# Expert retrieval in groups of 32 tokens with four heads side by side, and another order of key and weight transfers

## The reference

```python
h  = rmsnorm(x) * norm1 modulated by adaLN(c)            # 6 vectors of 1024 per request from c @ w_ada
z  = h @ w_in                                            # conv parts, q, k, v, indexer q, k, w, two gates
mix = sigmoid(ga) * (conv(z) @ w_convout) + sigmoid(gb) * (sparse_attention(z, cache) @ w_attnout)
x  = x + gate1 * (mix @ w_out)
h2 = rmsnorm(x) * norm2 modulated                        # the second half: retrieval
q  = (h2 @ w_q).reshape(t, 8 heads, 2, 128)              # w_q is 1024 x 2048
s  = q . sub_keys                                        # per head two lists of 128 scores
s1, i1 = top_k(s[:, :, 0], 16); s2, i2 = top_k(s[:, :, 1], 16)
e, g = best 16 of the 256 sums s1 + s2; e = i1 * 128 + i2; g = softmax(the 16 sums)
act = gelu(u_tab[e] . h2)                                # u_tab, v_tab: 16384 rows of 1024
y  = sum over 8 heads x 16 of (g * act) * v_tab[e]
out = x + gate2 * y
```

## Time and profile before

| | |
|---|---|
| median of three runs | 1093.47 us |
| the profiled execution | 1094.85 us, its span 1093.0 |
| TensorE busy | 950.8 us, 87% |
| VectorE busy | 715.6 us, 65% |
| ScalarE busy | 415.7 us, 38% |
| GpSimd busy | 286.2 us, 26% |
| moved from HBM | 377.75 MB, 347 GB/s over the span |
| queue of the gathers | 306.61 MB |

### The profile page before, as it was taken

How to read it: one execution, slowest core, us unless ns; L and a number is a source line. 1 busy time by engine, 2 the same in 40 slices (tenths; PEclk the granted TensorE clock), 3 DMA queues, 4 the chain that set the end, 5 groups by cost and what they waited for, 6 DMA issues and landing times.

```text
span 1093.0 us, 11438 instructions
## 1 busy us (share of the span) xinstructions
PE 950.8 (87%) x3288; PEld 487.2 (45%) x3288; DVE 715.6 (65%) x1775; ACT 415.7 (38%) x1120; POOL 286.2 (26%) x314
## 2 busy tenths in 40 slices
PE   4999999969999999999999877877877777777787
PEld 2457877646777655554454322322222222222222
DVE  1266879885647877676667787888864444444544
ACT  2112313101402555455466445345343333333333
POOL 0001000002001333343344333333333333333330
PEclk9999999989999999999999999899999999999999
DMA  9837352777536999999999999999999999999993
GB/s 367 326 120 263 116 198 87 251 294 273 194 127 259 390 416 418 421 420 419 421 419 420 420 419 421 420 419 419 420 420 420 421 420 420 420 419 420 421 420 152
DMA packets 63764, 380.08 MB, mean 348 GB/s; under 512 B 7651, under 2 KB 20115, under 8 KB 22358
## 3 DMA queue, kind: packets, MB, share of 16 engines
q0 software_dynamic: 42944, 306.61, 68.1%
q1 hardware_dynamic: 20470, 72.41, 17.6%
q10 hardware_dynamic: 288, 0.35, 0.1%
HBM read 377.75 MB, written 1.59 MB: 347 GB/s over the span
## 4 chain that ended last, share of the span: by engine, by line
DMA 44%; PE 41%; DVE 6%; ACT 4%; issue 2%; SPq 2%; POOL 0%; DVEq 0%; POOLq 0%; ACTq 0%
DMA big<-peer_uv,oT 39%; PE twoA L591 7%; PE twoD L956 7%; PE twoD L958 6%; PE twoA L895 4%; PE twoA L569 3%; PE twoD L829 3%; DMA big<-weight_rows 3%; DVE big L1851 2%; SPq L987 2%; DMA r<-peer_uv,oT 1%; PE twoD L817 1%; PE twoA L728 1%; PE twoA L511 1%; ACT big L1298 1%
## 5 line engine op out<-in xcount | busy, mean ns | idle before, releaser
L1089 POOL DMA_INDIRECT big<-peer_uv,oT x259 | 244.7, 945 | 484.8 <-PE twoD L958 379.2
L956 PE MATMUL twoD<-big 128*128 128x512 f32 x518 | 285.6, 633 | 98.2 <-ACT big L1298 98.1
L1851 DVE CUSTOM_DVE_ANT_0 big<-big,twoA 128x1024 f32<-128x1024 f32 x146 | 178.2, 1221 | 144.4 <-DMA big<-peer_uv,oT 143.1
L958 PE MATMUL twoD<-big 128*128 128x512 f32 x518 | 268.2, 600 | 0.0
L1293 ACT ACTIVATE oT<-oT,wsel 128x1 f32<-128x1 f32 x288 | 84.5, 293 | 323.0 <-DVE oT L1851 317.8
L956 PEld LDWEIGHTS twoD<-big 128*128 128x128 f32 x518 | 84.5, 191 | 269.8 <-ACT big L1298 232.8
L1851 DVE CUSTOM_DVE_ANT_0 big<-big,twoD 128x1024 f32<-128x1024 f32 x113 | 137.9, 1221 | 71.6 <-DMA big<-peer_uv,oT 68.8
L958 PEld LDWEIGHTS twoD<-big 128*128 128x128 f32 x518 | 99.7, 193 | 126.1 <-issue 126.1
L591 PE MATMUL twoA<-hT,big 128*128 128x288 f32 x448 | 115.3, 414 | 10.0 <-DMA big<-weight_rows 10.0
L1298 ACT ACTIVATE big<-ctab,oT 128x128 f32<-128x128 f32 x288 | 115.6, 401 | 9.5
L591 PEld LDWEIGHTS twoA<-hT,big 128*128 128x128 f32 x448 | 85.0, 193 | 36.7 <-DMA big<-weight_rows 10.9
(11 more groups left out here) (330 smaller groups left out, 952.5 us busy)
## 6 DMA issues: line engine op xcount, KB each, us to landing
big<-weight_rows SPq DMA_DIRECT2D x24, 2048.0 KB, 11.4
big<-weight_rows SPq DMA_DIRECT2D x8, 1024.0 KB, 4.9
big<-peer_uv,oT POOLq DMA_INDIRECT x259, 22.8
r<-key_rows SPq DMA_DIRECT2D x40, 64.0 KB, 2.0
big<-index_rows SPq DMA_DIRECT2D x64, 32.0 KB, 2.7
r<-weight_rows SPq DMA_DIRECT2D x1, 2048.0 KB, 12.1
big<-key_rows SPq DMA_DIRECT2D x24, 64.0 KB, 4.9
big<-weight_rows SPq DMA_DIRECT2D x1, 1312.0 KB, 14.3
```

The source lines that it names most:

```text
L956: pe.matmul(acc[0][:, :], diag[j % NDG], row[:, 0:512], start=(s == 0), stop=(s == SLOTS[t] - 1), skip_group_check=True)
L958: mm = pe.matmul(acc[1][:, :], diag[j % NDG], row[:, 512:D], start=(s == 0), stop=(s == SLOTS[t] - 1), skip_group_check=True)
L1089: pool.indirect_dma_start(pairs[home[i]], None, peer_uv, bass.IndirectOffsetOnAxis(ap=eidx[:, t, s:s + 1], axis=0)).then_inc(row_in[home[i ...
L1851: dve.tensor_tensor_reduce(out=row, in0=row, in1=h2tok[t][:, :], scale=1.0, scalar=0.0, op0=ALU.mult, op1=ALU.add, accum_out=dots[:, t, s: ...
```

## The change

1. **Groups.** All 288 tokens go in nine groups of 32, each with four heads in the four strips of 32 partitions: 9 x 32 slots, again 288 rounds. A unit is now four or eight heads of 32 tokens.
2. **Queries.** For group 0, `first_queries` computes rows: 32 tokens by 512 columns, in four strips, for two weight blocks at once, and turns them with `sum4`. Heads 0 to 3 come ahead of the first gather, 4 to 7 behind it. The sixteen blocks then run twice in the rounds: for tokens 32 to 127 in rounds 1 to 16, and for tokens 128 to 287 in every second round from 19 to 49.
3. **Values.** ScalarE writes a 128 x 32 matrix (`spread`); the two halves of v go to two neighbouring strips, other ones in the next round, and one PSUM bank holds a group's sums.
4. **h2** is spread to the four strips by 32 small matmuls per group (`spread_h2`), into one place, so it waits for the last dot of the group before.
5. **Group ends.** `scale_sums`, then `finish_group` adds the strips and x on TensorE; rows go out after every group.
6. **Ring.** 6 buffers, 8 from gather 27, 10 from 35, 12 from 43; the added ones lie in the weights `peerq` 0, 1 and 2.
7. **Transfers.** `peerq` 0 to 3 go to slots 0, 1, 5, 4 (before 5, 4, 0, 1). Keys of requests 0 and 1 are asked for after `convout`, of 2 and 3 after `gate` 7, of 7 after `adaG` 11.

```diff
-        ALL_ROWS, RING = 11, ((0, 7), (50, 9), (74, 11))
+        ALL_ROWS, RING = 12, ((0, 6), (27, 8), (35, 10), (43, 12))
-("peerq", 0, 5), ("peerq", 1, 4), ("peerq", 2, 0), ("peerq", 3, 1)]
+("peerq", 0, 0), ("peerq", 1, 1), ("peerq", 2, 5), ("peerq", 3, 4)]
-        BLOCK_AT = {4 + 6 * n: 5 + n for n in range(11)}
-        SCORE_AT = {5 + 12 * n: 2 + n for n in range(6)}
+        BLOCK_AT = {1 + n: (n, GTOK, P) for n in range(16)}
+        BLOCK_AT.update({19 + 2 * n: (n, P, TOK) for n in range(16)})
+        SCORE_AT = {17: 2}
+        SCORE_AT.update({GSLOTS * (n - 2) + 5: n for n in range(3, len(units))})
-            while unit < len(units) and i >= SCORED[unit] and n < (2 if unit < 4 else 1):
+            while unit < len(units) and i >= SCORED[unit] and n < (2 if unit < 3 else 1):
...
+            def first_queries(n):
+                for half in range(2):
+                    w, b = weights(pe, group("peerq", 2 * n + half)), A.open(pe)
+                    for k in range(DC):
+                        q = k % 4
+                        if n == 0:
+                            pe.wait_ge(h_ready, DC + k + 1)
+                        mm = pe.matmul(b[32 * q:32 * q + 32, :], hT[:, k, 0:GTOK], w[:, k, :], start=(k < 4), stop=(k >= 4),
+                                       skip_group_check=True)
+                    A.close(mm)
+                b = A.open(pe)
+                for half in range(2):
+                    pe.wait_ge(qrow_ready, 2 * n + half + 1)
+                    for j in range(4 * half, 4 * half + 4):
+                        mm = pe.matmul(b[:, GTOK * j:GTOK * (j + 1)], qrow[n][:, j * P:(j + 1) * P], cv["sum4"], start=True, stop=True)
+                A.close(mm)
+            first_queries(0)
             score_unit(0)
+            spread_h2(0)
...
+            first_queries(1)
+            score_unit(1)
...
+            def spread_h2(t):
+                if t:
+                    pe.wait_ge(u_used, GSLOTS * t)
+                for c in range(DC):
+                    for r in range(QUAD):
+                        mm = pe.matmul(h2rep[GTOK * r:GTOK * (r + 1), c * P:(c + 1) * P], hT[:, c, GTOK * t:GTOK * (t + 1)], ident,
+                                       start=True, stop=True)
...
+                if s == GSLOTS - 1 and t + 1 < GROUPS:
+                    spread_h2(t + 1)
+                pe.wait_ge(spread_ready, j + 1)
+                for half in range(2):
+                    r = (2 * j + half) % QUAD
+                    mm = pe.matmul(bankD[t % 2][GTOK * r:GTOK * (r + 1), :], spread[j % NDG],
+                                   pairs[home[j]][:, D + 512 * half:D + 512 * (half + 1)], start=(s < 2), stop=(s >= GSLOTS - 2),
+                                   skip_group_check=True)
                 mm.then_inc(v_used, 1)
...
+            def finish_group(t):
+                b = A.open(pe)
+                for c in range(DC):
+                    half = c // 4
+                    pe.matmul(b[GTOK * half:GTOK * (half + 1), c % 4 * P:(c % 4 + 1) * P], xT[:, c, GTOK * t:GTOK * (t + 1)], ident,
+                              start=(c % 4 == 0), stop=False, skip_group_check=True)
+                pe.wait_ge(ysum_ready, t + 1)
+                for half, of in enumerate(("even", "odd")):
+                    mm = pe.matmul(b[GTOK * half:GTOK * (half + 1), :], cv[of], ysum[:, t % 2, :], start=False, stop=True,
+                                   skip_group_check=True)
...
                 if g == group("convout"):
                     sp.wait_ge(*attended[0])
-                    for b in range(KB):
-                        load_keys(b)
+                    load_keys(0)
+                    load_keys(1)
+                if g == group("gate", 7):
+                    load_keys(2)
+                    load_keys(3)
+                if g == group("adaG", 1):
                     sp.wait_ge(a_ready, 1)
                     load_keys(NB - 1)
...
-                elif home[i] in (5, 6):
+                elif home[i] in (6, 7):
                     pool.wait_ge(*released[group("peerq")])
-                elif home[i] in (7, 8):
+                elif home[i] in (8, 9):
+                    pool.wait_ge(*released[group("peerq", 1)])
+                elif home[i] in (10, 11):
                     pool.wait_ge(*released[group("peerq", 2)])
-                elif home[i] in (9, 10):
-                    pool.wait_ge(*released[group("peerq", 3)])
```

More of the change, by code:

```diff
@@ L470, in layer_program @@
         NORM_AT = {ROUTED_AT[unit] + 3: unit for unit in range(1, len(units))}
+        assert all(ROUTED_AT[unit] + 3 <= first_slot[unit] for unit in range(1, len(units)))
         home, turn, before = [], [], []
@@ L861, in score_unit @@
-                A.close(mm)
-            def turn_h2(t):
-                pe.wait_ge(h_ready, 2 * DC + 2 if t else 2 * DC)
-                for q in range(DC):
-                    mm = pe.transpose(h2tok[t][:, q * P:(q + 1) * P], hT[:, q, t * P:(t + 1) * P], ident)
-                mm.then_inc(h2_ready, 1)
-            first = weights(pe, group("peerq"))
-            for j in range(2):
+                for i in range(nh):
+                    for r in range(QUAD):
+                        for q in range(2):
+                            head = QUAD * (h + i) + r
+                            mm = pe.matmul(b[GTOK * r:GTOK * (r + 1), (2 * i + q) * P:(2 * i + q + 1) * P],
+                                           qpT[:, 2 * head + q, GTOK * t:GTOK * (t + 1)], subT[:, q * PH + head, :], start=True, stop=True)
@@ L933, in _, with gate_rows @@
-            keep_busy(A, 4)
+                if end == TOK:
+                    released[g] = (a_full, A.n)
+            def gate_rows(t):
+                if t == 0:
+                    pe.wait_ge(bias_landed, 16)
+                    pe.wait_ge(g2sel_ready, 1)
+                    pe.wait_ge(adaG_ready, 2)
+                b = A.open(pe)
+                for r in range(QUAD):
+                    pe.matmul(b[GTOK * r:GTOK * (r + 1), :], g2sel[:, t * GTOK:(t + 1) * GTOK], adaG[:, r % 2, :], start=True, stop=False,
+                              skip_group_check=True)
+                for r in range(QUAD):
+                    mm = pe.matmul(b[GTOK * r:GTOK * (r + 1), :], ones[0:1, 0:GTOK], biasG[:, r % 2 * 512:(r % 2 + 1) * 512], start=False,
+                                   stop=True, skip_group_check=True)
+                A.close(mm)
@@ L1297, in weigh @@
                     act.wait_ge(v_used, j - NDG + 1)
[L1298 removed]
+                act.activation(spread[j % NDG], cv["sum4"], ACT.Copy, scale=w).then_inc(spread_ready, 1)
             def copy_query(j, a, e):
```

318 lines of the change are left out of this document (126 added, 192 removed).

## The result

| | before | changed |
|---|---|---|
| median of runs | 1093.28 us (1092.79 to 1094.33, 5 runs) | 1118.76 us (1118.33 to 1122.6, 5 runs) |
| profiled execution, its span | 1094.85, 1093.0 us | 1122.6, 1120.8 us |
| first gather issued | 347.54 | 345.18 |
| last dot, on the last gather's data | 1083.21 | 1110.77 |
| from the one to the other | 735.7 | 765.6 |

The changed kernel is slower: ratio 1.0238, 95% interval 1.0227 to 1.0249. The forecast was 1102.5 us with a range of 1088 to 1112; the direction was right, the size was not, and the time lies outside the range. The terms in the profiled executions: start of the retrieval -2.4, retrieval +29.9, tail +0.2, which is the 27.75 us between 1094.85 and 1122.6. So nearly all of the miss lies in the retrieval, where +11.4 (1.7 + 9.7) had been forecast.

The account below looks back on a forecast made before the run. Bound: gather transfers at 2.55 us each, TensorE ahead of them. Terms -4.8 + 2.0 + 1.7 + 9.7 + 0.4 = +9.0 gave 1103.9 us profiled, 1102.5 as median; range 1088 to 1112.

Parts of the forecast that it names:

- start of the retrieval: Up to the first gather: -4.8 us from the closed hole at the front, +2.0 us from the new query computation.
- tail: Last landing to end: 9.2 to 9.8 us, or 3.4 longer at half clock; +0.4 us taken.
- 1.7 + 9.7: Retrieval: 1.7 us lost in the early rounds with query blocks, 9.7 us at the three ring growths (4.0, 3.4, 2.3).
- the cover at the growth waits: Gathers 27, 35, 43: slack of gathers already issued covers 7.65 of the first hold's 9.85 us, leaving 2.2 dry.
- 7.65 of slack: Six buffers: 6 x 2.55 - 2.55 - 3.4 (landing to buffer reuse) - 1.7 (issue to data) us.
- 1.8 for VectorE: First growth: VectorE, with two routing steps a round, is up to 2.5 us late by round 24; 1.8 taken.
- the spread at 1 us of delay: Second growth: dot 32 waits for 32 spreading matmuls behind dot 31, about 1 us late; 3.4 us in all.
- The front's step: Ahead of the sample scores: moving keys closes TensorE's 9.96 us hole; gain 6.9, net -4.8 us after the cold clock.
- the 2.1 charged: Score matmuls: the new TensorE wait of 5.1 us can cool the clock, 2.1 us charged (bounds 0 and 4).
- rivals 2 and 3: Rounds: changes between whole-array and strip matmuls stop TensorE, 1108, chance 0.08; two strips don't overlap, about 1130, chance 0.05.
- Rival 1: Gathers 27, 35, 43: the queue still holds enough and TensorE keeps up before, 1091.1 us, chance 0.29.
- rival 4: Front: the hole closes but another wait (keys 7, adaG) keeps TensorE until 269, 1107.3 us, chance 0.08.

Follow-up runs that it names:

- the repeat: The changed kernel run once more, unaltered: 1117.39 us, ratio 1.0215.
- nothing held: The changed kernel with the ring growing at gathers 31, 39 and 47 instead of 27, 35 and 43: 1095.29 us, ratio 1.0016.
- halved routing: The changed kernel with half of VectorE's routing of the second group left out: 1114.0 us, ratio 1.0176.
- moved gate rows: The changed kernel with the gate rows in rounds 26 and 28 instead of 22 and 24: 1122.1 us, ratio 1.0253.
- both at once: The changed kernel with the halved routing and the moved gate rows together: 1111.6 us, ratio 1.0169.
- the order alone: The kernel before with only the key transfers in the new order: 1090.6 us, ratio 0.9972.
- the kernel with the ten matmuls: The kernel before with the new key order and ten matmuls that nothing reads ahead of the wait for the sample mask: 1087.55 us, ratio 0.9938.

## Why the prediction was wrong

**The failed step is the cover at the growth waits.** The prediction put the hold of gather 27 at 9.85 us. The issues measure it: 81.8 us behind gather 0 in the repeat, 70.9 with nothing held, 10.9 us. That was near. Against it stood "7.65 of slack", which assumes values that end 3.4 us behind their data, and 1.8 for VectorE: 4.0 us dry. This cover wasn't there. With no gather issued, the dry stretch is the time from the landing of gather 26 to the values of round 24, then the block, then 1.7 us to data. In the change (VectorE's dot of round 24, then TensorE with gate rows, values 24 and the block of round 25):

```profile
424.38 1.20 DVE L1867 CUSTOM_DVE_ANT_0 big<-big,twoD 128x1024 f32<-128x1024 f32 x1
...
425.37 0.60 PE L972 MATMUL twoD<-r,big 128*32 128x512 f32 x2
425.39 1.44 PE L936 MATMUL twoA<-r,qkbuf 128*32 128x512 f32 x6
426.76 1.06 PE L939 MATMUL twoA<-r,ones 1*32 1x512 f32 x8
427.75 1.05 PE L972 MATMUL twoD<-big 128*32 128x512 f32 x4
428.73 2.44 PE L922 MATMUL twoA<-hT,big 128*128 128x160 f32 x16
```

Gather 26 had landed at 424.7, when the DMA share fell; the values of round 24 ended at 428.8, the block at 431.2. By the prediction's figures the values would have ended 0.1 us behind that landing (3.4 + 1.8 - 2 x 2.55); they ended 4.1 behind it. 4.1 + 2.4 + 0.3 (from the block's end to the issue) + 1.7 = 8.5, and 8.2 was measured, against 4.0. At the second growth the values of round 32 ended at 457.7, 3.3 behind the landing of gather 34, and 7.7 us were dry against 3.4; at the third, 0.9 behind, and 4.9 against 2.3. The terms were each too small by 2.6 to 4.3 us, and their sum, 9.7, should have been 20.8.

Two causes of the lag at the first growth are shown. From 412 to 433 VectorE was busy all but 0.14 us, dots and routing, and the values waited for it; the prediction had allowed 1.8. And the gate rows had no term: they held TensorE 1.8 us each in rounds 22 and 24 (from 425.97, the end of the values of round 23, to 427.75). The halved routing, the moved gate rows and both at once show that the two stand side by side: 0.7 and 0.1 us off the repeat's dry stretch singly, 3.2 together. With both gone the values of round 24 ended at 420.4, just as gather 26 had landed (about 420.5), which is the prediction's figure, and 4.2 us were dry, where it had 4.0. TensorE's timeline of that kernel, the values of round 24 and the block of round 25:

```profile
419.36 1.05 PE L972 MATMUL twoD<-big 128*32 128x512 f32 x4 [0.88 <-ACT big L1314]
420.34 2.44 PE L922 MATMUL twoA<-hT,big 128*128 128x160 f32 x16
```

The prediction also used the full slack again at gather 27, after setting 5.6 us of TensorE's lag in rounds 1 to 16 against it. That was careless, but it isn't what cost the time: with those blocks thinned the values of round 24 still ended 4.1 us behind the landing of gather 26, and the dry stretch was 7.6.

At the second growth there is a third: the spreading of h2 for the next group (L878) stands behind the block of round 31 on TensorE. The block of round 29 before it had run at half clock, 4.13 us instead of 2.44.

```profile
444.92 4.13 PE L922 MATMUL twoA<-hT,big 128*128 128x160 f32 x16
...
449.97 2.44 PE L922 MATMUL twoA<-hT,big 128*128 128x160 f32 x16
452.34 1.95 PE L878 MATMUL twoD<-ctab,hT 128*32 128x128 f32 x64
```

The prediction had put the spread at 1 us of delay; VectorE stood 4.91 us for it before dot 32, which came at 454.36. The clock's part in this is small: with TensorE kept busy the second wait was 0.9 us shorter than in the repeat. What the order of spread and block costs by itself wasn't tried.

**What was right.** With nothing held, the other terms can be read by themselves (profiled 1095.55): start -2.2, forecast -2.8; retrieval from first issue to last dot 738.3 against 735.7, +2.6, forecast +1.7; tail 10.2 against 9.8, +0.4 as forecast. They sum to +0.8, and 1094.85 + 0.8 is 1095.6. The front's step holds as told: hole closed, idle of 4.98 (forecast 5.1), scores at 262.63 (262.6), and the cold clock is paid in the score matmuls. Its price isn't fixed. Where the clock came back behind the first half, as in the profile of the change, the start was close to the sum (-2.4 against -2.8). Where both halves ran cold, as in the repeat and with the order alone, it was 2.0 us more than that: the kernel with the ten matmuls started its gathers 4.35 us earlier than the one with the order alone, against the 2.1 charged, and the order alone gave 3.2 us where the sum had 4.8. Value matmuls in two strips took 1.05 us and blocks with values 2.94 a round, both as worked out; rivals 2 and 3 fell with that. Rival 1, no starvation, fell at the three growths, and rival 4 with the scores at 262.63. The Trainium skill (TensorEngine Tiling (Array Packing), Key Properties) has a change of tiling mode drain TensorE; in 2.94 us rounds against 2.9 worked out without a drain, no cost of it is seen.

**What stays open**: of the 18.5 us by which the retrieval of the profiled change missed (29.9 against 11.4), 11.1 are the dry stretches, 3.4 ScalarE's stall and 0.9 the rest of the retrieval. Some 3 us are left, the same 3 by which the growth cost more (23 to 24) than its dry stretches. Open are also the stall itself; ScalarE's stall; and why the clock came back behind the first half of the scores in some executions and behind the second in others. The order of the query weights and the spreading of h were not tried by themselves.

## What to carry to other kernels

Where an in-order queue feeds the bottleneck, a wait in it costs what is not covered by work already issued, and that cover must be counted at that very moment: take how far the consumers lag behind their data there, and add every other user of their engines in those rounds. Two delays that run side by side hide each other, so an experiment that takes away one of them can show nothing. Let a ring grow only where its own turn comes later than the last reader of the new buffer; four rounds made 23 us here. A wait that is moved to an idle TensorE is paid once more in the matmuls behind it, and a few matmuls that nothing reads ahead of it were worth nearly as much as the edit itself (3.0 and 3.2 us).

## What the runs showed of the hardware

- After 4.88 us idle TensorE's granted clock stood at 0.50 and stayed low although TensorE then worked with hardly a gap; it was at 1.00 again only behind 272. The repeat shows the same, but the change, after an idle of 4.98 us and with the same matmuls, ran its second half of scores from 267.65 on at full clock: 2.0 us of start between two executions of one kernel. The windows of the kernel with the order of keys alone (columns as above):

```profile
262.00:265.00 3.00, 2.56 (x11) 0.67 (x15) 0.76 (x3) 0.00 (x0) 0.00 (x0) 0.50 0.00 0
265.00:273.00 8.00, 8.00 (x38) 2.34 (x31) 2.01 (x6) 1.93 (x6) 0.00 (x0) 0.55 0.00 0
273.00:276.00 3.00, 2.64 (x16) 1.92 (x14) 2.43 (x9) 1.43 (x4) 0.00 (x0) 1.00 0.00 0
```

  Ten matmuls of 288 columns in the idle time, and it was 1.00 from 240 to 275; that was worth 3.0 us of time (1090.6 to 1087.55).
- ScalarE stood still for 3 to 6 us in some executions while the first gathers were under way, and not in others of the same kernel, with its input ready (5.24 us in the change, none in its repeat); gather 6 moved by 3.4 us with it.
